# GpSimd adds one more piece of half B's sum of squares at three norm boundaries, and TensorE sums one source one step later

## The chip, the cores and the metric

The kernel runs on one core of a Trainium2 chip. The metric is the device time of one launch in microseconds. Before the change the median of 3 runs is 1094.82 us, and the runs lie between 1094.5 and 1095.06 us.

## The reference, cut to what matters

Two transformer-like layers work on 512 tokens of width 1024. Each layer is a mixer (a recurrent branch with stick-breaking attention in layer 0, windowed attention in layer 1) and a gated conv-FFN. Every one of the four has a norm before it and a norm behind it, so that between two of them stands this pair:

```python
x = x + rms_norm(m, norm_mix_post[layer])
h = rms_norm(x, norm_ffn_pre[layer])
...
def rms_norm(x, g):
    y = xf * lax.rsqrt(jnp.mean(xf * xf, axis=-1, keepdims=True) + RMS_EPS) * g
```

The change touches only the mean of squares of `m`, the output of a mixer or an FFN, for the second half of the tokens.

## The kernel before, in words

Activations lie transposed: 8 tiles (`DT`) of 128 features by 512 tokens (`T`). Every product of activations and weights is done as three matmuls (high by high, low by high, high by low part, lines 1673 to 1675). ScalarE makes the high part of a weight block (`w_hi`, L725), VectorE the low part (`w_lo`, L1122, a subtraction of two SBUF tiles of 128x2048).

There are three boundaries (`bi` = 0, 1, 2): behind mixer 0, behind FFN 0 and behind mixer 1. Boundary 0 lies at about 185 to 237 us of the span, boundary 1 at 540 to 603 us, boundary 2 at 700 to 751 us. At each, the tokens are worked in two halves of 256, A and B, so that half A's norm runs while TensorE still computes half B's last matmuls. Half B's norm then runs while TensorE starts the next projection on half A (`first_units`: two units `j` = 0, 1 of eight steps `k`, six 256-column matmuls a step, first for half A, which I call phase A, then for half B, phase B, which goes through `k` with both units in a step of twelve matmuls).

The chain of half B's norm is this, with the line in brackets:

1. ScalarE squares the last block of half B as two pieces of 256 columns: the lower feature tile into `sq[:, 0:HALF]` (L750, counted by `psq_done`), the upper one into `sq[:, HALF:T]` (L751, counted by `psq_last`). Both hold the same 256 tokens.
2. GpSimd adds the lower piece to the running sum `sumsq` (L692, counted by `psum_done`). In half A it adds the upper piece as well (L696; at boundary 2 VectorE does half A's two adds).
3. TensorE sums over the 128 features with a column of ones (L1750). In half B it takes two sources for each of two token blocks, `sumsq` and the upper piece of `sq`: four matmuls. They stand ahead of step 5 of unit 0 in phase A.
4. ScalarE takes the root (L757), VectorE the reciprocal (L1153), and builds a diagonal matrix (L1156). TensorE spreads it with a matmul of ones (L1760) ahead of step 7 of unit 0.
5. VectorE splits a weight block (L1122; at boundary 1 two half blocks of L1128 around the reciprocal), then for each feature tile normalises (L1443), adds to `x` (L1449) and, with ScalarE's `hx_hi` (L941), makes `hx_lo` (L1453). TensorE's phase B waits for `hx_lo` of each `k`.

Ahead of item 4's reciprocal, VectorE's program has another split of a weight block (L1122 with `splits[0]`) at boundaries 0 and 2. Engines take their instructions in program order; the order here is written out by hand.

Of the kernel before, what the change touches and what calls it, by code (L numbers as in the profile page):

```python
# [17 lines left out]
ALU = mybir.AluOpType  # L18
# [3 lines left out]
P = 128  # L22
T = 512
# [36 lines left out]
HALF = T // 2  # L60
# [9 lines left out]
def group_of(u):  # L70

    shift = 0
    for layer in range(2):
        if u >= U_DOWN[layer] + N_DOWN:
            shift += G_SHIFT
        elif u >= U_DOWN[layer]:
            return U_DOWN[layer] - shift + (u - U_DOWN[layer]) // len(DOWN_K)
    return u - shift
# [18 lines left out]
def post_squares(bi):  # L97

    return 8 * bi


def post_sums(bi):

    return (0, 12, 12 + 8)[bi]


def last_square(bi, h):

    return 6 + h if bi == 1 else 4 + 3 * h


def pre_sums(p):

    return (DT - 1) * p


def a_halves(bi):

    return (0, 3, 4)[bi]
# [7 lines left out]
def evacuated(g):  # L127

    return g + 1 - N_IN if g < G_QKV else g + 1 - N_IN - N_QKV
# [24 lines left out]
def build(nc, io, out):  # L154
    es = ExitStack()

    def sem(name):
        return es.enter_context(nc.semaphore(name))
# [5 lines left out]
    def at(name, shape, dt, offset):  # L164
        return nc.alloc_sbuf_tensor_at(name, shape, dt, offset=offset)
# [11 lines left out]
    def place(name, shape, dt):  # L177
        t = at(name, shape, dt, where[0])
        where[0] += size(shape, dt)
        return t  # L180
# [17 lines left out]
    ident, ones = (const[:, P * i:P * i + P] for i in range(2))  # L198
# [17 lines left out]
    sumsq = place("sumsq", [P, T], F32)  # L216
# [16 lines left out]
    sq = [at(f"sq{b}", [P, T], F32, tmp0 + (0, 2, 3)[b] * T * 4) for b in range(3)]  # L233
# [105 lines left out]
    def bank(b, n=1):  # L339
        return ps[:, T * b:T * (b + n)]  # L340
# [18 lines left out]
    def tokens_of(h):  # L359

        return slice(HALF * h, HALF * h + HALF)
# [37 lines left out]
    def sb_set(h):  # L399
# [21 lines left out]
    psq_done, psum_done, pms_mm, pstd_done, prcol_done, pdiag_done, pbc_mm = (sem(n) for n in (  # L421
        "psq_done", "psum_done", "pms_mm", "pstd_done", "prcol_done", "pdiag_done", "pbc_mm"))
    ahalf_mm, ahalf_evac = sem("ahalf_mm"), sem("ahalf_evac")
    psq_last = sem("psq_last")
# [226 lines left out]
    @block.gpsimd  # L651
    def _(pool):
        def pre_norm(p):

            for i in range(1, DT):
                pool.wait_ge(sq_done, DT * p + i + 1)
                if i == 1:
                    if p:
                        pool.wait_ge(pms_mm, 2 * p)
                    ins = pool.tensor_tensor(sumsq[:], sq[0][:], sq[1][:], ALU.add)  # L660
                else:
                    pool.wait_ge(sum_done, pre_sums(p) + i - 1)
                    ins = pool.tensor_tensor(sumsq[:], sumsq[:], sq[i % 2][:], ALU.add)
                ins.then_inc(sum_done, 1)

        def whole_sums(bi, n):

            for i in range(1, n):
                pool.wait_ge(psq_done, post_squares(bi) + i + 1)
                if i == 1:  # L670
                    pool.wait_ge(ms_mm, bi + 1)
                    ins = pool.tensor_tensor(sumsq[:], sq[0][:], sq[1][:], ALU.add)
                else:
                    pool.wait_ge(psum_done, post_sums(bi) + i - 1)
                    ins = pool.tensor_tensor(sumsq[:], sumsq[:], sq[i % 3][:], ALU.add)
                ins.then_inc(psum_done, 1)

        def half_sums(bi, h):

            for j in range(2):  # L680
                q = 2 + 3 * h + j
                pool.wait_ge(psq_done, post_squares(bi) + q + 1)
                for b in range(2):
                    pool.wait_ge(psum_done, post_sums(bi) + 1 + 6 * h + 2 * j + b)
                    pool.tensor_tensor(sumsq[:, tokens_of(h)], sumsq[:, tokens_of(h)], sq[q % 3][:, tokens_of(b)], ALU.add).then_inc(psum_done, 1)

        def last_sum(bi, h):

            q = last_square(bi, h)
            pool.wait_ge(psq_done, post_squares(bi) + q + 1)  # L690
            pool.wait_ge(psum_done, post_sums(bi) + (5 + 2 * h if bi == 1 else 5 + 6 * h))
            pool.tensor_tensor(sumsq[:, tokens_of(h)], sumsq[:, tokens_of(h)], sq[q % 3][:, 0:HALF], ALU.add).then_inc(psum_done, 1)  # L692
            if h == 0:
                pool.wait_ge(psq_last, 2 * bi + 1)
                pool.wait_ge(psum_done, post_sums(bi) + 6)
                pool.tensor_tensor(sumsq[:, 0:HALF], sumsq[:, 0:HALF], sq[q % 3][:, HALF:T], ALU.add).then_inc(psum_done, 1)  # L696

        pre_norm(0)
        whole_sums(0, 2)
        half_sums(0, 0)  # L700
        last_sum(0, 0)
        half_sums(0, 1)
        last_sum(0, 1)
        pre_norm(1)
        whole_sums(1, 6)
        last_sum(1, 0)
        last_sum(1, 1)
        pre_norm(2)
        whole_sums(2, 2)
        half_sums(2, 0)  # L710
        half_sums(2, 1)
        last_sum(2, 1)
        pre_norm(3)
# [956 lines left out]
    def _(pe):  # L1670
# [6 lines left out]
        def unit_ready(u, i=None):  # L1677

            pe.wait_ge(w_lo_done, u + 1 if i is None else i * RING + (u + 1))
# [56 lines left out]
        def post_mean_square(bi, h):  # L1736

            if h:
                pe.wait_ge(pstd_done, 2 * bi + 1)
            else:  # L1740
                pe.wait_ge(std_done, bi + 1)
            pe.wait_ge(psum_done, post_sums(bi) + (7 + h if bi == 1 else 7 + 5 * h))
            if h:
                pe.wait_ge(psq_last, 2 * bi + 2)
            q = last_square(bi, h)
            for t in (2 * h, 2 * h + 1):
                c = P * (t - 2 * h)
                srcs = (sumsq[:, P * t:P * t + P], sq[q % 3][:, HALF + c:HALF + c + P])[0:h + 1]
                for i, src in enumerate(srcs):
                    last = pe.matmul(bank(7)[:, t:t + 1], src, ones[:, 0:1], start=i == 0 and t == 2 * h, stop=i == h and t == 2 * h + 1)  # L1750
            last.then_inc(pms_mm, 1)

        def post_spread(bi, h):

            pe.wait_ge(pdiag_done, 2 * bi + h + 1)
            if h:
                pe.wait_ge(pstd_done, 2 * bi + 2)
            elif bi == 2:
                pe.wait_ge(ahalf_evac, a_halves(2) + 3)
            pe.matmul(bank(6 + h)[:, 0:HALF], ones, diag[:, 2 * h:2 * h + 2, :].rearrange("p t c -> p (t c)"),  # L1760
                      start=True, stop=True).then_inc(pbc_mm, 1)
# [190 lines left out]
        def first_half(u, h, k):  # L1952

            for b in range(2):
                dst = bank(group_banks(group_of(u)) + h)[:, tokens_of(b)]
                ins = three(dst, *weights(u, k, b), hx_hi[:, k, tokens_of(h)], hx_lo[:, k, tokens_of(h)], k == 0 and b == 0,
                            k == UK - 1 and b == 1)
            return ins
# [82 lines left out]
        def first_units(bi, u):  # L2041

            a_copied, evac = a_halves(bi) + (1 if bi == 1 else 3), evacuated(group_of(u) - 1)
            pe.wait_ge(ahalf_evac, a_copied)
            for j in range(2):
                unit_ready(u + j)
                for k in range(UK):
                    if j == 0 and k == 5:
                        post_mean_square(bi, 1)
                    if j == 0 and k == 7:  # L2050
                        post_spread(bi, 1)
                    pe.wait_ge(hx_ready, DT + 2 * DT * bi + k + 1)
                    first_half(u + j, 0, k)
            pe.wait_ge(group_evac, evac)
            for k in range(UK):
                pe.wait_ge(hx_ready, 2 * DT + 2 * DT * bi + k + 1)
                for j in range(2):
                    last = first_half(u + j, 1, k)
                    if k == UK - 1:
                        last.then_inc(unit_done, 1)  # L2060
            if bi == 1:
                banks_free(group_of(u + 2))
                unit_ready(u + 2)
                tokens(u + 2, group_banks(group_of(u + 2)),
                       {(0, 2): lambda: mean_square(2), (1, 4): lambda: spread(2)}).then_inc(unit_done, 1)
            else:
                unit(u + 2, hx, hooks={(0, 1): lambda: mean_square(bi + 1), (0, 6): lambda: spread(bi + 1)})
# [147 lines left out]
        ffn(0, 0)  # L2215
        down_halves()
        first_units(1, U_QKV)
        unit(U_QKV + 3, hx)
        unit(U_QKV + 4, hx, hooks={
# [119 lines left out]
```

## Time and profile before

| What | Value |
|---|---|
| median of 3 runs | 1094.82 us |
| profiled execution, device time | 1095.11 us |
| its span in the trace | 1093.3 us |
| TensorE matmul busy | 1083.1 us, 99% of the span |
| VectorE busy | 691.2 us, 63% |
| ScalarE busy | 501.8 us, 46% |
| GpSimd busy | 69.9 us, 6%, 62 instructions |
| granted TensorE clock | 1.00 of full speed over the span |

The profiled execution is 1.81 us longer than its span and 0.29 us above the median. A matmul's row begins when it starts and its length includes the pipeline's drain, so the distance from start to start is what a matmul costs the engine. A record on the row of TensorE is one pass: these float32 matmuls of one column show two records each.

### The profile page before, as it was taken

Reading aid. Unit: us, or ns where it says so; the run is one execution under the profiler, and the core shown is the slowest. Engines: PE = TensorE matmul, PEld = TensorE weight load, DVE = VectorE, ACT = ScalarE, POOL = GpSimd, SP = SyncE. Lnnn points to the kernel's source line nnn. Section 1 sums busy time; section 2 is a strip of 40 time slices with the busy share of each in tenths; the row PEclk is TensorE's granted clock in tenths of the full one; section 3 lists DMA queues with packets and bytes.
Section 4 is the critical chain, followed back from the end, with each engine's and each line's share of the span. In section 5 each row is a group of like instructions: output and inputs, shape, how many; then the busy total and the mean of one; then the engine's idle time right before and its main releaser. Section 6 shows DMA issues by size and latency. Waiting matters only on the chain.

```text
span 1093.3 us, 15107 instructions
## 1 busy us (share of the span) xinstructions
PE 1083.1 (99%) x5998; PEld 918.3 (84%) x5998; DVE 691.2 (63%) x920; ACT 501.8 (46%) x714; POOL 69.9 (6%) x62
## 2 busy tenths in 40 slices
PE   9999999999999999999999999999999999999997
PEld 7886889998888888888899877998888888888886
DVE  7675777788776767622257777398876767661313
ACT  6556966555343444322235466454444444441321
POOL 3000001230000000001103000121000000000000
PEclk9999999999999999999999999999999999999999
DMA  6323232213222222223322623212222222221322
GB/s 230 116 78 77 78 116 78 78 43 112 82 111 86 106 89 103 83 91 106 107 81 82 166 94 116 83 73 78 85 108 89 104 92 100 97 96 58 116 97 77
DMA packets 22919, 105.49 MB, mean 96 GB/s; under 512 B 4048, under 2 KB 6480, under 8 KB 12240
## 3 DMA queue, kind: packets, MB, share of 16 engines
q1 hardware_dynamic: 22720, 104.71, 28.1%
q8 instruction: 40, 0.66, 0.2%
q14 instruction: 15, 0.12, 0.0%
q10 hardware_dynamic: 144, 0.01, 0.0%
HBM read 98.02 MB, written 2.10 MB: 92 GB/s over the span
## 4 chain that ended last, share of the span: by engine, by line
PE 92%; DVE 4%; ACT 2%; DMA 1%; issue 1%; SPq 1%; DVEq 0%
PE ps L1673 29%; PE ps L1675 28%; PE ps L1674 28%; PE ps L1856 1%; PE ps L1869 1%; PE ps L1892 1%; DVE ps L1443 1%; PE ps L2162 1%; DVE x L1449 1%; PE ps L2173 1%; DVE hx_lo L1453 1%; DVE w_lo L1169 1%; PE ps L2189 1%; ACT w_hi_s L725 1%; ACT prob L1075 0%
## 5 line engine op out<-in xcount | busy, mean ns | idle before, releaser
L1673 PE MATMUL ps<-hx_hi,w_hi 128*128 128x512 f32 x812 | 320.0, 394 | 1.0 <-DVE w_lo L1169 0.9
L1675 PE MATMUL ps<-hx_hi,w_lo 128*128 128x512 f32 x812 | 316.4, 390 | 0.0
L1674 PE MATMUL ps<-hx_lo,w_hi 128*128 128x512 f32 x812 | 316.3, 390 | 0.0
L1122 DVE TENSOR_TENSOR w_lo<-w_raw,w_hi 128x2048 fp32r<-128x2048 f32 (+1 forms) x74 | 167.7, 2266 | 122.1 <-ACT w_hi L725 121.9
L725 ACT ACTIVATE w_hi<-w_raw 128x2048 fp32r<-128x2048 f32 (+1 forms) x76 | 142.0, 1870 | 109.0 <-DMA w_raw<-in_ffn_w_down 90.7
L1673 PEld LDWEIGHTS ps<-hx_hi,w_hi 128*128 128x128 f32 x812 | 152.4, 188 | 38.0 <-issue 6.5
L1675 PEld LDWEIGHTS ps<-hx_hi,w_lo 128*128 128x128 f32 x812 | 152.4, 188 | 31.9
L1674 PEld LDWEIGHTS ps<-hx_lo,w_hi 128*128 128x128 f32 x812 | 152.5, 188 | 31.0 <-issue 0.5
L984 ACT ACTIVATE cg<-ug,vec 128x512 f32<-128x512 f32 x44 | 35.9, 816 | 140.7 <-DVE ug L1489 140.7
L996 ACT ACTIVATE g_hi<-cv 128x512 f32 (+1 forms) x44 | 27.8, 632 | 111.1 <-DVE cv L1507 111.1
L1498 DVE SCALAR_TENSOR_TENSOR cg<-ug,vec,cg 128x511 f32<-128x511 f32 x88 | 65.8, 748 | 20.4 <-ACT cg L984 20.4
L1489 DVE TENSOR_TENSOR ug<-ps,rbc 128x512 f32<-128x512 f32 x44 | 30.4, 690 | 61.4 <-PE ps L1675 61.3
L1673 PE MATMUL ps<-w_hi,g_hi 128*128 128x512 f32 x176 | 68.9, 391 | 0.0
L1675 PE MATMUL ps<-w_hi,g_lo 128*128 128x512 f32 x176 | 68.5, 389 | 0.0
L1674 PE MATMUL ps<-w_lo,g_hi 128*128 128x512 f32 x176 | 68.5, 389 | 0.0
L1498 DVE SCALAR_TENSOR_TENSOR cv<-uv,vec,cv 128x511 f32<-128x511 f32 x88 | 65.8, 748 | 0.0
L1509 DVE TENSOR_TENSOR g_lo<-cv,g_hi 128x512 f32 (+1 forms) x44 | 30.5, 693 | 37.0 <-ACT g_hi L996 37.0
L1674 PE MATMUL ps<-g_lo,w_hi 128*128 128x512 f32 x132 | 51.4, 389 | 0.0
L1675 PE MATMUL ps<-g_hi,w_lo 128*128 128x512 f32 x132 | 51.4, 389 | 0.0
L1673 PE MATMUL ps<-g_hi,w_hi 128*128 128x512 f32 x132 | 51.4, 389 | 0.0
L941 ACT ACTIVATE hx_hi<-x,vec 128x256 fp32r<-128x256 f32 x48 | 24.0, 506 | 33.9 <-DVE x L1449 33.9
L1675 PEld LDWEIGHTS ps<-w_hi,g_lo 128*128 128x128 f32 x176 | 33.0, 188 | 6.9
(284 smaller groups left out, 1948.9 us busy)
## 6 DMA issues: line engine op xcount, KB each, us to landing
w_raw<-in_ffn_w_up SPq DMA_DIRECT2D x40, 1024.0 KB, 4.8
w_raw<-in_ffn_w_down SPq DMA_DIRECT2D x16, 1024.0 KB, 4.8
w_raw<-in_even_w_in SPq DMA_DIRECT2D x6, 1024.0 KB, 4.9
w_raw<-in_even_w_out SPq DMA_DIRECT2D x3, 1024.0 KB, 4.8
w_raw_s<-in_odd_w_qkv SPq DMA_DIRECT2D x3, 1024.0 KB, 4.8
w_raw<-in_odd_w_qkv SPq DMA_DIRECT2D x3, 1024.0 KB, 5.4
w_raw<-in_odd_w_o SPq DMA_DIRECT2D x3, 1024.0 KB, 5.4
rsw<-rp SPq DMA_DIRECT2D x40, 64.0 KB, 2.0
```

What stands on the lines that cost most here:

```text
L725: act.activation(w_hi[buffer(u)][:, 0:k], w_raw[buffer(u)][:, 0:k], ACT.Copy).then_inc(w_hi_done, 1)
L941: act.activation(hx_hi[:, i, tokens_of(h)], x[:, i, tokens_of(h)], ACT.Identity, scale=gain(which, layer, i)).then_inc(hx_hi_done, 1)
L984: act.activation(cg[:], ug[:], ACT.Identity, scale=col(ffn_vec(layer, 2, j)), bias=col(ffn_vec(layer, 3, j))).then_inc(center, 1)
L996: act.activation(tile_(g_hi, j), cv[:], ACT.Copy).then_inc(g_hi_done, 1)
L1122: dve.tensor_tensor(w_lo[s][:, 0:k], w_raw[s][:, 0:k], w_hi[s][:, 0:k], ALU.subtract).then_inc(w_lo_done, 1)
L1169: dve.tensor_tensor(w_lo[u][:, ks], w_raw[u][:, ks], w_hi[u][:, ks], ALU.subtract).then_inc(piece_signal(n, first_lo, w_lo_done), 1)
L1489: dve.tensor_tensor(halves(ug[:]), out_tile(u, b0, 0), halves(rbc[:]), ALU.mult).then_inc(scaled, 1)
L1498: dve.scalar_tensor_tensor(out=dst[:, s:], in0=src[:, 0:T - s], scalar=col(ffn_vec(layer, 2 - s, j + FT * b)), in1=dst[:, s:], op0=ALU.mul ...
L1509: dve.tensor_tensor(tile_(g_lo, j), cv[:], tile_(g_hi, j), ALU.subtract).then_inc(g_ready, 1)
L1673: pe.matmul(dst, s_hi, r_hi, start=first, stop=False)
L1674: pe.matmul(dst, s_hi, r_lo, start=False, stop=False)
L1675: return pe.matmul(dst, s_lo, r_hi, start=False, stop=last)
```

## The change

In half B, too, GpSimd adds the upper piece of the last square to `sumsq`, at all three boundaries. TensorE then sums only `sumsq`, with two matmuls where there were four, and no longer waits for `psq_last`; it waits for one more GpSimd add. The counts in `post_sums` follow. The sum is moved from ahead of step 5 to ahead of step 6 of unit 0, the spread from ahead of step 7 of unit 0 to ahead of step 0 of unit 1.

```diff
 def post_sums(bi):
-    return (0, 12, 12 + 8)[bi]
+    return (0, 13, 13 + 9)[bi]
...
-            if h == 0:
-                pool.wait_ge(psq_last, 2 * bi + 1)
-                pool.wait_ge(psum_done, post_sums(bi) + 6)
-                pool.tensor_tensor(sumsq[:, 0:HALF], sumsq[:, 0:HALF], sq[q % 3][:, HALF:T], ALU.add).then_inc(psum_done, 1)
+            pool.wait_ge(psq_last, 2 * bi + h + 1)
+            pool.wait_ge(psum_done, post_sums(bi) + (6 + 2 * h if bi == 1 else 6 + 6 * h))
+            pool.tensor_tensor(sumsq[:, tokens_of(h)], sumsq[:, tokens_of(h)], sq[q % 3][:, HALF:T], ALU.add).then_inc(psum_done, 1)
...
-            pe.wait_ge(psum_done, post_sums(bi) + (7 + h if bi == 1 else 7 + 5 * h))
-            if h:
-                pe.wait_ge(psq_last, 2 * bi + 2)
-            q = last_square(bi, h)
+            pe.wait_ge(psum_done, post_sums(bi) + (7 + 2 * h if bi == 1 else 7 + 6 * h))
             for t in (2 * h, 2 * h + 1):
-                c = P * (t - 2 * h)
-                srcs = (sumsq[:, P * t:P * t + P], sq[q % 3][:, HALF + c:HALF + c + P])[0:h + 1]
-                for i, src in enumerate(srcs):
-                    last = pe.matmul(bank(7)[:, t:t + 1], src, ones[:, 0:1], start=i == 0 and t == 2 * h, stop=i == h and t == 2 * h + 1)
+                last = pe.matmul(bank(7)[:, t:t + 1], sumsq[:, P * t:P * t + P], ones[:, 0:1], start=t == 2 * h, stop=t == 2 * h + 1)
...
-                    if j == 0 and k == 5:
+                    if j == 0 and k == 6:
                         post_mean_square(bi, 1)
-                    if j == 0 and k == 7:
+                    if j == 1 and k == 0:
                         post_spread(bi, 1)
```

On TensorE, at boundary 2, phase A, the sum stood after five steps of unit 0. Steps of unit 0 read `w_hi_x_148`; the rows below are the last matmul of step 4, the sum, and the first of step 5:

```order
L1675 MATMUL ps<-hx_hi,w_lo_x_146 128x256
L1750 MATMUL ps<-const,sumsq 128x1
L1750 MATMUL ps<-const,sq_86 128x1
L1750 MATMUL ps<-const,sumsq 128x1
L1750 MATMUL ps<-const,sq_86 128x1
L1673 MATMUL ps<-hx_hi,w_hi_x_148 128x256
```

Now six steps of unit 0 stand ahead of it, and it has two matmuls, which the print joins in one row (lines are seven lower in the changed file from here on, and one lower for the three matmuls of a product):

```order
L1674 MATMUL ps<-hx_hi,w_lo_x_146 128x256
L1743 MATMUL ps<-const,sumsq 128x1 x2
L1672 MATMUL ps<-hx_hi,w_hi_x_148 128x256
```

The six matmuls of step 5 have moved ahead of the sum, and the two with `sq_86` are gone.

The spread, on the same engine and at the same boundary, stood ahead of step 7, the last one of unit 0 (`w_hi_x_148`), with unit 1 (`w_hi_s_154`) behind it:

```order
L1760 MATMUL ps<-diag,const 128x256
L1673 MATMUL ps<-hx_hi,w_hi_x_148 128x256
L1674 MATMUL ps<-hx_lo,w_hi_x_148 128x256
L1675 MATMUL ps<-hx_hi,w_lo_x_146 128x256
L1673 MATMUL ps<-hx_hi,w_hi_x_148 128x256
L1674 MATMUL ps<-hx_lo,w_hi_x_148 128x256
L1675 MATMUL ps<-hx_hi,w_lo_x_146 128x256
L1673 MATMUL ps<-hx_hi,w_hi_s_154 128x256
```

Now unit 1 begins right behind it:

```order
L1672 MATMUL ps<-hx_hi,w_hi_x_148 128x256
L1673 MATMUL ps<-hx_lo,w_hi_x_148 128x256
L1674 MATMUL ps<-hx_hi,w_lo_x_146 128x256
L1753 MATMUL ps<-diag,const 128x256
L1672 MATMUL ps<-hx_hi,w_hi_s_154 128x256
```

Both pieces have two steps, twelve matmuls, between the sum and the spread, as before. On GpSimd, at boundaries 1 and 2 half B's second add follows the first directly (`sumsq` is the running sum, `sq_86` the buffer of the last square; L660 begins the next norm's sum):

```order
 L692 TENSOR_TENSOR sumsq<-sumsq,sq_86 128x256
+L695 TENSOR_TENSOR sumsq<-sumsq,sq_86 128x256
 L660 TENSOR_TENSOR sumsq<-sq_85,sq_86 128x512
```

VectorE's, ScalarE's and the queues' orders are as before.

## Rows read from the trace of the kernel before

**Rows 1.** The page, part 1: busy time, share of the span, instructions.
```profile
PE 1083.1 (99%) x5998; PEld 918.3 (84%) x5998; DVE 691.2 (63%) x920; ACT 501.8 (46%) x714; POOL 69.9 (6%) x62
```
**Rows 2.** Windows, 716 to 724 us: busy us and instructions by engine, clock, DMA.
```profile
716.00:724.00 8.00, 8.00 (x71) 8.00 (x70) 7.37 (x17) 6.27 (x13) 2.28 (x3) 1.00 0.38 131
```
**Rows 3.** Timeline, TensorE, boundary 0: start, length, engine, line, operation, tiles [idle before].
```profile
210.98 0.35 PE L1750 MATMUL ps<-const,sumsq 128*128 128x1 f32 x2
...
211.87 0.36 PE L1673 MATMUL ps<-hx_hi,w_hi_x 128*128 128x256 f32 x1
...
227.18 0.28 PE L1673 MATMUL ps<-hx_hi,w_hi_x 128*128 128x256 f32 x1
```
**Rows 4.** Timeline, GpSimd, boundary 0, both halves' last adds.
```profile
192.47 0.74 POOL L692 TENSOR_TENSOR sumsq<-sumsq,sq 128x256 f32<-128x256 f32 x1 [2.62 <-ACT sq L750]
193.35 0.74 POOL L696 TENSOR_TENSOR sumsq<-sumsq,sq 128x256 f32<-128x256 f32 x1
...
208.08 2.80 POOL L692 TENSOR_TENSOR sumsq<-sumsq,sq 128x256 f32<-128x256 f32 x1 [1.32 <-ACT sq L750]
```
**Rows 5.** Timeline, VectorE, boundary 0, half B.
```profile
208.00 2.28 DVE L1122 TENSOR_TENSOR w_lo_s<-w_raw_s,w_hi_s 128x2048 fp32r<-128x2048 f32 x1
212.34 0.17 DVE L1153 RECIPROCAL rcol<-std 128x2 f32<-128x2 f32 x1 [2.06 <-ACT std L757]
...
226.15 0.77 DVE L1453 SCALAR_TENSOR_TENSOR hx_lo<-x,vec,hx_hi 128x256 fp32r<-128x256 f32 x1
```
**Rows 6.** Timeline, ScalarE, boundary 0, the root of half B.
```profile
212.04 0.26 ACT L757 ACTIVATE std<-ps,narrow 128x2 f32<-128x2 f32 x1 [1.47 <-PE ps L1750]
```
**Rows 7.** Timeline, TensorE, boundary 1: the sum, the spread, phase B's k = 5.
```profile
576.23 0.28 PE L1750 MATMUL ps<-const,sumsq 128*128 128x1 f32 x2
...
578.77 0.70 PE L1760 MATMUL ps<-diag,const 128*128 128x256 f32 x2
...
592.74 0.28 PE L1673 MATMUL ps<-hx_hi,w_hi_s 128*128 128x256 f32 x1
```
**Rows 8.** Timeline, VectorE, boundary 1: reciprocal, diagonal, `hx_lo` of k = 5.
```profile
578.04 0.16 DVE L1153 RECIPROCAL rcol<-std 128x2 f32<-128x2 f32 x1
578.23 0.48 DVE L1156 TENSOR_SCALAR diag<-const,rcol 128x128 f32<-128x128 f32 x2
...
590.00 0.70 DVE L1453 SCALAR_TENSOR_TENSOR hx_lo<-x,vec,hx_hi 128x256 fp32r<-128x256 f32 x1
```
**Rows 9.** Timeline, GpSimd, boundary 1, half B's last add.
```profile
574.38 0.77 POOL L692 TENSOR_TENSOR sumsq<-sumsq,sq 128x256 f32<-128x256 f32 x1 [15.95 <-ACT sq L750]
```
**Rows 10.** Timeline, GpSimd, boundary 2, half B's last add.
```profile
723.26 0.77 POOL L692 TENSOR_TENSOR sumsq<-sumsq,sq 128x256 f32<-128x256 f32 x1 [1.15 <-ACT sq L750]
```
**Rows 11.** Timeline, VectorE, boundary 2: split, reciprocal, `hx_lo` of k = 4 and 5.
```profile
723.35 2.83 DVE L1122 TENSOR_TENSOR w_lo_s<-w_raw_s,w_hi_s 128x2048 fp32r<-128x2048 f32 x1
726.10 0.15 DVE L1153 RECIPROCAL rcol<-std 128x2 f32<-128x2 f32 x1
...
737.86 1.26 DVE L1453 SCALAR_TENSOR_TENSOR hx_lo<-x,vec,hx_hi 128x256 fp32r<-128x256 f32 x1
...
739.89 0.76 DVE L1453 SCALAR_TENSOR_TENSOR hx_lo<-x,vec,hx_hi 128x256 fp32r<-128x256 f32 x1
```
**Rows 12.** Timeline, TensorE, boundary 2: sum, spread, phase B's k = 4 and 5.
```profile
724.12 0.35 PE L1750 MATMUL ps<-const,sumsq 128*128 128x1 f32 x2
...
726.82 0.70 PE L1760 MATMUL ps<-diag,const 128*128 128x256 f32 x2 [0.15 <-DVE diag L1156]
...
739.17 0.39 PE L1673 MATMUL ps<-hx_hi,w_hi_x 128*128 128x256 f32 x1
...
740.71 0.38 PE L1673 MATMUL ps<-hx_hi,w_hi_x 128*128 128x256 f32 x1
```
**Rows 13.** Timeline, GpSimd and VectorE near the span's start, both busy.
```profile
16.01 1.56 POOL L663 TENSOR_TENSOR sumsq<-sumsq,sq 128x512 f32<-128x512 f32 x1
...
16.34 1.78 DVE L1173 SCALAR_TENSOR_TENSOR hx_lo<-x,vec,hx_hi 128x512 fp32r<-128x512 f32 x1
```

## The prediction

> **What bounds the kernel now.** I read four views in this order. First the busy times [rows 1]: TensorE is busy 99% of the span, so an edit pays only if it removes TensorE time or a TensorE stall, and costs whatever it makes TensorE wait. Second a stretch of TensorE alone, for its pace: 71 matmuls of 256 columns in 8.00 us at full granted clock, 0.113 us each, so a step of six is 0.68 us [rows 2]. Third TensorE's timeline at each boundary, for distances from start to start; only one wait is marked in brackets there, 0.15 us ahead of the spread at boundary 2 [rows 12], but the distances show smaller and unmarked gaps. Fourth the timelines of GpSimd, VectorE and ScalarE there, because half B's norm is a chain through all of them that TensorE meets again in phase B, at each k of `hx_lo`. The question at each boundary is which comes last in phase B, TensorE itself or that chain. The chain's clock starts at the end of the sum.
>
> At boundary 2 it is the chain: `hx_lo` of k = 4 ends at 737.86 + 1.26 = 739.12 [rows 11] and TensorE's k = 4 starts at 739.17; `hx_lo` of k = 5 ends at 740.65, TensorE starts it at 740.71 [rows 12]. At boundary 0 it is TensorE by a little: `hx_lo` of k = 5 ends at 226.92 and could be used 0.05 later, 226.97 [rows 5], TensorE starts k = 5 at 227.18 [rows 3], so the chain has 0.21 us of room. At boundary 1 it has 592.74 - (590.70 + 0.05) = 1.99 us [rows 7, 8].
>
> **What goes from TensorE.** Four matmuls take from 210.98 to 211.87, 0.89 us [rows 3], or 0.22 each. Two go at each of three boundaries: 0.45 us less each. Phase A's steps cost 0.68 us each [rows 2], two of them 1.36.
>
> **What the move does.** Standing one step later and being 0.45 shorter, the sum ends 0.68 - 0.45 = 0.23 us later if nothing makes it wait. The spread, two steps behind it, is due 0.23 later too, with one more step done. Nothing on the queues moves, no DMA is issued at another place.
>
> **What GpSimd's add costs.** It is off TensorE, but TensorE now waits for it. The same pair of adds in half A: 192.47, then 193.35, 0.74 us long [rows 4], so the second starts 0.14 after the first ends and adds 0.88. But GpSimd and VectorE stand in each other's way when both read two SBUF tiles. Near the start, GpSimd's add takes 1.56 us and VectorE's `hx_lo` from 16.34 takes 1.78 and ends at 18.12, 0.55 after the add ends at 17.57 [rows 13]: one at a time. At boundary 0 the half-B add starts at 208.08, 0.08 behind a VectorE split of 2.28 us, and takes 2.80 instead of 0.74; it ends at 210.88, 0.60 after the split [rows 4, 5]. At boundary 2 the add wins by 0.09 and takes 0.77; the split behind it takes 2.83 instead of 2.28 [rows 10, 11]: it could begin about 0.55 late, near 723.90, and holds GpSimd off to its end at 726.18.
>
> **Boundary 0.** First add ends 210.88 (as before). Second: 211.02 to 211.76; VectorE is idle for 2.06 us ahead of 212.34 [rows 5], so nothing blocks it. TensorE starts a sum 0.10 us after the add's end (210.88 to 210.98) [rows 3, 4]: 211.86. Without the wait it would start at 210.98 + 0.68 = 211.66. So it waits 0.2, is through at 212.31, where before its next step 6 began at 211.87 + 0.68 = 212.55: TensorE is 0.24 ahead. The root before began at 212.04, 1.06 after the sum's start [rows 6]; with two matmuls fewer it follows 0.61 after the start: 212.47, 0.43 later. Reciprocal, diagonal, split, normalising and `hx_lo` follow 0.43 later; the second add ends before the diagonal is built and meets no two-tile work of VectorE. The chain had 0.21 of room at k = 5, so TensorE leaves phase B 0.43 - 0.21 = 0.22 later. **+0.22 us.**
>
> **Boundary 1.** First add 574.38 to 575.15 [rows 9], second to 576.03; TensorE comes at 576.23 + 0.68 = 576.91 [rows 7], so it does not wait. The root starts at 576.91 + 0.61 (worked out at boundary 0) = 577.52 and is usable 0.30 after (212.04 to 212.34) [rows 5, 6], at 577.82. The reciprocal stands directly behind a half split of VectorE, with no idle time, at 578.04 [rows 8], so it stays. Diagonal ready at 578.71, spread before at 578.77 [rows 7, 8]. Before, TensorE came there after two steps (576.23 + 0.89 + 1.36 = 578.48) and stood 0.29. Now it comes at 576.91 + 0.45 + 1.36 = 578.72 and spreads at the same 578.8 with a whole step more done. So it gains 0.68, with 1.99 of room for the chain in phase B, and keeps it. **-0.68 us.**
>
> **Boundary 2.** First add ends 724.03, the second is issued about 724.17, while the split has held since 723.90. By the row of boundary 0 it ends 0.60 after the split: 726.78; TensorE starts the sum at 726.88, where before it started at 724.12 [rows 12] and now was due at 724.80. Behind it on TensorE waits all of phase A's rest: it stands 2.1 us. Root at 726.88 + 0.61 = 727.49, reciprocal 0.30 later, 727.79, against 726.10 [rows 11]: +1.69. VectorE, ready at 726.18, stands still until then with the whole chain behind. The spread is due at 726.88 + 0.45 + 1.36 = 728.69, behind the diagonal (0.18 + 0.48 after the reciprocal, as in [rows 8]: 728.45), so the 0.15 us wait there goes; it pays nothing, since phase B's k = 4 and k = 5 hang on the chain. Its `hx_lo` move by 1.69, TensorE's k = 5 from 740.71 to 742.40. **+1.69 us.**
>
> What TensorE gains in phase A (0.45 and the spread's wait) is used up there.
>
> **The sum.** 0.22 - 0.68 + 1.69 = +1.23 us. On the profiled execution 1095.11 + 1.23 = 1096.34; that execution is 0.29 above the median, so on the median 1094.82 + 1.23 = 1096.05, say 1096.0 us. I take 0.2% as what a measurement can tell from no change, here 2.2 us; the forecast is a small loss inside it.
>
> The unknown is the grant: no row shows two adds of GpSimd with a 2.28 us split issued between them. Lower bound for boundary 2: the second add is not held up at all (0.88 as in half A); upper: held up for the whole of the split. Rows 13, where the two engines alternate although GpSimd's next add is ready, are the nearest, and they say held up. I take the upper one.
>
> Two pages bear on this. The Trainium skill (SBUF — State Buffer, Who interferes with whom) says that whichever of the two engines issues first holds their common port pair for the whole instruction. By that, as by the rows, the split issued at 723.35 goes ahead of an add issued at 724.17. The Trainium skill (Perfetto Trace Analysis, GPSIMD Engine Instruction) warns that a GpSimd row's length is unreliable and to go by spacing. By spacing an add costs 0.88 where the row says 0.74; TensorE's start 0.10 behind the drawn end shows that the ends can be used here.
>
> **Rivals.**
> - *No port trouble at boundary 2.* GpSimd's second add slips in or beside: ends 724.91, TensorE sums at 725.01, 0.2 late; the root follows at 725.62 as before, the chain does not move, boundary 2 gives 0. If in addition the add at boundary 0 is only 0.2 late as worked out, the sum is 0.22 - 0.68 + 0 = -0.46: 1094.4 us, on the faster side though within 0.2%. For it: the two adds are only 0.14 apart. Against: rows 13 and the split's 0.55 us stretch.
> - *The add goes first, the split pays.* Same 725.01 for the sum, but the split is held until about 724.8 and ends at 727.0 instead of 726.18: chain +0.85 at boundary 2. Sum +0.4: 1095.2 us. It needs GpSimd to take the port twice running over a waiting VectorE, which rows 13 speak against.
> - *Boundary 1's gain is lost.* Between boundaries 1 and 2 other engines end the attention steps; if one of them does not move along with TensorE, the 0.68 goes and the sum is +1.9: 1096.7. Against: everything there starts from TensorE's results behind the boundary.
> - *The stall costs clock.* The granted clock is 1.00, 2.4 GHz, ahead of boundary 2 [rows 2]. If 2.1 us of standing made it fall to 1.2 GHz, each 0.113 us matmul would cost 0.113 more: 20 of them add 2.3 us and bring 1098.3. No row shows a stall of that length, for or against.
>
> **How the numbers follow.** Forecast 0.68; no port trouble 0.11; split pays 0.07; gain of boundary 1 lost 0.09; clock 0.05. The forecast's own range is 1095.6 to 1096.5. Adding the first two on one side and the third on the other, and 0.3 us for the spread of the runs, the range is 1094.7 to 1097.1. Faster by over 0.2% would need -2.2 us, more than the three boundaries can give (3 x 0.68): 0.02. Slower by over 0.2% (above 1097.0) takes the clock case and the upper tail of the others: 0.12. The rest, 0.86, is within 0.2%.
>
> **What would show each step.** At boundary 2 GpSimd's second add of half B some 2.5 us long, ending 0.6 behind the split; a TensorE wait of some 2 us on it ahead of the sum; VectorE idle about 1.6 us ahead of its reciprocal. At boundary 0 the root about 0.43 later counted from its half-B first square. At boundary 1 no gap ahead of the spread. Counted from boundary to boundary, TensorE's distance should be +0.2, -0.7, +1.7. If the second add at boundary 2 is 0.74 us long, the forecast is wrong and the first two rivals decide.

## The result, and the profile after

The changed kernel takes 1098.34 us in the median of 8 runs (1097.84 to 1100.28), the kernel before 1095.0 us (1094.5 to 1095.58, 8 runs): ratio 1.0032, interval [1.0022, 1.0043], 3.3 us slower. Measured once more beside the kernel before, it is 1098.89 against 1095.27 us (1.0035, [1.0021, 1.0048]). The forecast was 1096.0 us and the range ended at 1097.1, so the time lies outside it.

The page after; it answers to [rows 1]. The span is 3.1 us longer, TensorE is busy 0.2 us less, GpSimd 4.1 us more:

```profile
span 1096.4 us, 15086 instructions
PE 1082.9 (99%) x5986; PEld 918.0 (84%) x5986; DVE 691.3 (63%) x920; ACT 502.2 (46%) x714; POOL 74.0 (7%) x65
```

So much of the loss is waiting. Some of it must be slower matmuls, though: six one-column matmuls are gone, by the forecast 3 x 0.45 us, and the busy time fell by 0.2. TensorE's waits after, whole span (in total, times, longest, us):

```profile
PE ps L1743 <- POOL sumsq L695: 2.2, 2, 2.0
...
PE ps L1672 <- DVE w_lo_s L1121: 1.0, 1, 1.0
PE ps L1753 <- DVE w_lo_s L1127: 0.9, 1, 0.9
...
PE ps L1672 <- DVE hx_lo L1452: 0.4, 1, 0.4
```

Four new ones. The first two numbers of the first line are one wait of 2.0 at boundary 2 and one of 0.2 at boundary 0, on the added add. The second and third lines are both at boundary 1, which the prediction had as a gain. The fourth, 0.37 us, is at boundary 0, in phase B at k = 4 (225.93).

**Boundary 2.** GpSimd, VectorE and TensorE after, three timelines (start, length, instruction, idle before). They answer to [rows 10 to 12]; the whole place has come 0.76 us later:

```profile
724.02 0.76 POOL L692 TENSOR_TENSOR sumsq<-sumsq,sq 128x256 f32<-128x256 f32 x1 [1.16 <-ACT sq L749]
724.93 2.59 POOL L695 TENSOR_TENSOR sumsq<-sumsq,sq 128x256 f32<-128x256 f32 x1
```

```profile
724.11 2.83 DVE L1121 TENSOR_TENSOR w_lo_s<-w_raw_s,w_hi_s 128x2048 fp32r<-128x2048 f32 x1
728.57 0.17 DVE L1152 RECIPROCAL rcol<-std 128x2 f32<-128x2 f32 x1 [1.64 <-ACT std L756]
```

```profile
727.66 0.58 PE L1743 MATMUL ps<-const,sumsq 128*128 128x1 f32 x4 [2.00 <-POOL sumsq L695]
...
731.19 0.41 PE L1672 MATMUL ps<-hx_hi,w_hi_s 128*128 128x256 f32 x1
```

The added add is 2.59 us long and ends at 727.52, 0.58 behind the split's end at 726.94. The reciprocal moves from 726.10 to 728.57, which is 1.71 later counted from the first add. The last row shows what I had given a chance of 0.05: some 2 us behind the stall a 256-column matmul takes 0.41 us in its row, and they start 0.21 apart, not 0.113. The windows after show the clock (stretch, its length, busy of TensorE, weight loads, VectorE, ScalarE, GpSimd, then granted clock, DMA):

```profile
728.00:730.00 2.00, 2.00 (x16) 2.00 (x16) 1.39 (x4) 0.26 (x1) 0.00 (x0) 0.86 0.00 0
730.00:732.00 2.00, 2.00 (x9) 1.81 (x9) 1.97 (x3) 0.00 (x0) 0.00 (x0) 0.50 0.03 8
732.00:734.00 2.00, 2.00 (x16) 2.00 (x15) 1.93 (x5) 1.66 (x4) 0.00 (x0) 0.78 0.00 0
```

0.50 is 1.2 GHz: 9 matmuls in 2 us, where [rows 2] has 71 in 8.

**Boundary 1.** VectorE and TensorE after; they answer to [rows 7, 8]:

```profile
579.07 1.22 DVE L1127 TENSOR_TENSOR w_lo_s<-w_raw_s,w_hi_s 128x1024 fp32r<-128x1024 f32 x1
581.08 0.49 DVE L1442 SCALAR_TENSOR_TENSOR ps<-m,vec,ps 128x256 f32<-128x256 f32 x1 [0.79 <-PE ps L1753]
...
594.81 3.38 DVE L1121 TENSOR_TENSOR w_lo_s<-w_raw_s,w_hi_s 128x2048 fp32r<-128x2048 f32 x1
```

```profile
580.34 0.70 PE L1753 MATMUL ps<-diag,const 128*128 128x256 f32 x2 [0.87 <-DVE w_lo_s L1127]
...
598.34 0.35 PE L1672 MATMUL ps<-w_hi_s,hx_hi 128*128 128x256 f32 x1 [0.96 <-DVE w_lo_s L1121]
```

The spread is not waiting for the diagonal. It waits for a weight block, because "ahead of step 0 of unit 1" is written behind `unit_ready(u + j)` of unit 1, and the last half of those weights' low part is made by the half split at 579.07, which comes after the diagonal. VectorE in turn waits 0.79 us for the spread.

**Boundary 0.** The added add takes 0.73 us, and the reciprocal, at 212.34 in [rows 5], is 0.50 later:

```profile
211.05 0.73 POOL L695 TENSOR_TENSOR sumsq<-sumsq,sq 128x256 f32<-128x256 f32 x1
```

```profile
212.84 0.17 DVE L1152 RECIPROCAL rcol<-std 128x2 f32<-128x2 f32 x1 [2.53 <-ACT std L756]
```

### The profile page after: what moved, and what is told of

It reads as the page before. It is cut to its first block, busy times and chain, and to the rows that moved or that the text cites. A ratio compares the mean times of both kernels' runs of the same rounds, so it can differ in the third digit from the quotient of the medians.

```text
span 1096.4 us, 15086 instructions
## 1 busy us (share of the span) xinstructions
PE 1082.9 (99%) x5986; PEld 918.0 (84%) x5986; DVE 691.3 (63%) x920; ACT 502.2 (46%) x714; POOL 74.0 (7%) x65
## 4 chain that ended last, share of the span: by engine, by line
PE 90%; DVE 5%; ACT 2%; issue 1%; DMA 1%; POOL 1%; SPq 1%; DVEq 0%; POOLq 0%
PE ps L1672 28%; PE ps L1674 27%; PE ps L1673 27%; DVE ps L1442 1%; DVE hx_lo L1452 1%; DVE x L1448 1%; PE ps L1849 1%; PE ps L1862 1%; PE ps L1885 1%; PE ps L2155 1%; PE ps L2166 1%; DVE w_lo L1168 1%; DVE w_lo_s L1121 1%; PE ps L2182 1%; ACT w_hi_s L724 1%
## 5 line engine op out<-in xcount | busy, mean ns | idle before, releaser
L672 POOL TENSOR_TENSOR sumsq<-sq,sq 128x512 f32<-128x512 f32 x3 | 4.2, 1398 | 518.5 <-ACT sq L752 518.5
```

## Where the time is lost, by stretch

For every traced kernel I took two starts at each boundary, half B's first add on GpSimd (L692) and the next norm's sum on TensorE (first matmul of L1733 in the kernel before), and compared their distance with that in the kernel before (24.04, 23.40 and 22.35 us). The attention column runs from boundary 1's second start to the first square of boundary 2 (103.13 us before); no kernel here changes an instruction in it. Each value is from one profiled execution, in us against before; the last column is the difference of the medians, from 11 runs unless said.

| kernel | boundary 0 | boundary 1 | attention | boundary 2 | medians |
|---|---|---|---|---|---|
| the change | +0.40 | +0.91 | -0.59 | +2.31 | +3.34 (8 runs) |
| the change again | +0.40 | +0.93 | +0.04 | +1.76 | +3.62 (5 runs) |
| e1, boundary 0 only | +0.24 | | -0.49 | | +0.11 |
| e2, boundary 1 only | | +0.93 | -0.45 | | +0.64 |
| e3, boundary 2 only | | | +0.16 | +1.75 | +2.02 |
| e4, boundary 2, late sum | | | -0.66 | +1.78 | +1.53 |
| e5, boundary 1, spread first | | +0.01 | -0.19 | | -0.07 |
| e6, boundary 2, split halved | | | -0.56 | +0.67 | +0.92 |
| e7, move without add | +0.23 | +1.21 | -0.55 | +0.01 | +1.34 |
| e8, add without move | +0.25 | +0.04 | -0.22 | +3.58 | +3.81 (5 runs) |
| e9, repaired | +0.24 | +0.03 | +0.96 | +0.02 | +0.32 |
| e10, add goes first | | | -0.15 | +1.07 | +1.52 |
| e11, half split later | | | +0.43 | -0.16 | +0.52 |

The empty cells are stretches whose program is that of before; they read between -0.01 and +0.04, but for boundary 0 in e5 (-0.24) and e6 (-0.18), so a single value of 0.2 at boundary 0 proves little by itself; there the five kernels that have the change or a part of it all read +0.23 to +0.40.

These differences go with something that no edit here makes: at a granted clock of 1.00, TensorE runs its 256-column matmuls at one of two paces. The same stretch of boundary 0 in the kernel before and in e5, which has the same program there:

```profile
216.00:224.00 8.00, 8.00 (x71) 8.00 (x69) 7.79 (x15) 5.21 (x10) 4.08 (x4) 1.00 0.00 0
```

```profile
216.00:224.00 8.00, 8.00 (x73) 8.00 (x72) 7.79 (x15) 5.22 (x10) 3.94 (x4) 1.00 0.00 0
```

From start to start a matmul takes 0.118 us in the first and 0.113 us in the second and in e6. Over this half the quick pace brings TensorE up to the chain of the norm and gains it about the chain's 0.21 us of room. It also parts +0.40 from +0.24 where the program is the same: from the wait at k = 4 to the next norm's sum the change takes 6.60 us at the slow pace, e1 6.44 us at the quick one. What sets the pace stays open.

The attention stretch moves by -0.66 to +0.96 between executions of the same instructions. There TensorE waits for a chain of small DMAs. The chain that ended last has this last landing in the kernel before and after (start, us, what):

```profile
666.35 3.16 DMA rsw<-rp
```

```profile
667.72 2.54 DMA rsw<-rp
```

Up to the start of that landing the two traces take the same time from boundary 1's second start (68.57 and 68.60 us), so the 0.62 us between the landings is the 0.59 that the profile after seems to give back. In the change again the stretch reads +0.04, so it is luck of one execution, not an effect of the change, and the boundaries have to be read apart.

## The experiments

**e1, e2, e3: one boundary each.** The count of `post_sums`, the add, the one-source sum and the places are those of the change for one value of `bi` and those of before for the others:

```diff
-            if h == 0:
+            if h == 0 or bi in (2,):
...
-                    if j == 0 and k == 5:
+                    if (j, k) == {0: (0, 5), 1: (0, 5), 2: (0, 6)}[bi]:
```

> The change made at boundary 0 alone. Theory: the second add lies behind a first add that a VectorE split holds up, so half B's sum ends about 0.5 us later, the chain of the norm follows 0.5 us later, and 0.1 to 0.2 us of that is room: +0.3 to +0.4 us against before, no lower granted clock. Rival (each boundary costs a third of the measured 3.3 us, as a price of the change itself): +1.1 us.

> The change made at boundary 1 alone. Theory: the spread now stands behind TensorE's wait for unit 1's weights, whose low part VectorE finishes only after the diagonal; chain +0.9 us and the first matmul of the third unit, which waits for the last split of the chain, +0.9; the attention stage behind it may give back up to 0.6 where a DMA of the rotary swap lands earlier: +0.3 to +1.0 us. What the prediction said of this boundary: -0.7 us. Rival (a third each): +1.1 us.

> The change made at boundary 2 alone. Theory: the second add is held up by the split (2.6 us long instead of 0.74), TensorE stands 2 us, the chain is 1.7 us later, and the clock that drops behind the stall costs another 0.6 us: +2.1 to +2.6 us, with a stretch of a few us at half the granted clock near 727 to 731 us. Without the clock's share it would be +1.7. Rival (a third each): +1.1 us.

Measured: 1095.24, 1095.77 and 1097.15 us against 1095.13, so +0.1, +0.6 and +2.0; ratios 1.0002 [0.9993, 1.0011], 1.0005 [0.9996, 1.0014] and 1.0019 [1.0010, 1.0028]. Only the third is clear by its interval; for the first two the trace has to speak, and it shows +0.24 and +0.93 at the boundaries named and nothing at the others. By the traces thirds of 1.1 us are out; the medians' intervals alone would allow them. The medians add to 2.8 us against the 3.3 and 3.6 of the whole, within what the intervals allow; the stretches without any loss of clock add to 0.40 + 0.92 + 1.76 = 3.1.

In e3 TensorE stood 2.0 us on the add as in the change, but the clock stayed up in this execution:

```profile
728.00:730.00 2.00, 2.00 (x17) 1.94 (x16) 1.89 (x4) 0.04 (x1) 0.00 (x0) 1.00 0.03 8
730.00:732.00 2.00, 2.00 (x20) 2.00 (x19) 1.93 (x4) 0.15 (x1) 0.00 (x0) 1.00 0.00 0
```

So the expectation of a stretch at half clock was wrong for this execution, and boundary 2 costs 1.75 without it, against 2.31 with it. TensorE itself lost more than that 0.56 in the trace of the change: its first matmul of phase B starts 13.08 us behind half B's first add, in e3 11.48, so the slow stretch cost it 1.6 us. But in e3 it then stands about 1.0 us in waits for the norm's chain, which is equally late in both traces. That much of the loss is hidden.

**e4: the same add, the sum where TensorE has work.** Boundary 2 alone; sum ahead of step 1 of unit 1, spread ahead of step 3:

```diff
+                    if (j, k) == {0: (0, 5), 1: (0, 5), 2: (1, 1)}[bi]:
...
+                    if (j, k) == {0: (0, 7), 1: (0, 7), 2: (1, 3)}[bi]:
```

> At boundary 2 alone, GpSimd's second add as in the change, but the sum stands ahead of step 1 of unit 1 and the spread ahead of step 3, so that TensorE has work while the add is held up. Theory: no stall over 0.3 us, granted clock 1.00 throughout, the sum starts at the same 726.9 us and the chain is 1.7 us late as before: +1.5 to +1.8 us, so 0.6 less than the change at boundary 2 alone; that difference is the clock's share. Rival (the clock costs nothing that the chain does not cost anyway): the same as the change at boundary 2 alone, within 0.2 us. Rival (the stall itself, not the chain, is the cost): near 0.

Measured 1096.66 us, +1.5 (1.0015 [1.0006, 1.0024]). The add on GpSimd is as long as ever:

```profile
723.56 2.60 POOL L696 TENSOR_TENSOR sumsq<-sumsq,sq 128x256 f32<-128x256 f32 x1
```

TensorE now has no wait on it, but the missing time turns up in phase B, as three waits for `hx_lo`, 1.3 us in all, and the boundary costs +1.78, what it cost in e3. The stall itself is not the price: a stall that is filled is paid again where the chain is met. The medians of the two differ by 0.5 us, which is the size expected for the clock's share, but with these intervals the medians do not show it.

The mean clock of a run says little here. It is 1.000 or 0.999 in e4's 11 runs and 0.997 or 0.998 in nine of e3's 11, but the profiled execution of e3 has 0.998 with no fall at boundary 2: its clock falls at 1091.8 us, behind the last matmul, where it costs nothing:

```profile
1092.00:1094.00 2.00, 0.00 (x0) 0.00 (x0) 0.85 (x2) 0.00 (x0) 0.00 (x0) 0.50 0.48 180
```

That end stretch takes 0.00 to 0.16% off the mean in the 14 traces. Means of 0.997 and less stand only in kernels whose TensorE stalls for 2 us or more, four times in e3's 11 runs. That speaks for falls at boundary 2 in those executions, but no trace of them shows it.

**e5: the spread ahead of the weights at boundary 1.**

```diff
             for j in range(2):
+                if j == 1 and bi == 1:
+                    post_spread(bi, 1)
                 unit_ready(u + j)
```

> Boundary 1 alone, with the spread put ahead of TensorE's wait for unit 1's weights, everything else as in the change. Theory: the spread starts at 578.8 us as before the change, the chain does not move, and TensorE's gain of 0.7 us in phase A ends in a longer wait at the third unit, whose weights VectorE splits at the end of the chain with 0.1 us of room: 0 us against before, within 0.2. Rival (the prediction's own view, room of 2 us, gain kept): -0.7 us.

Measured 1095.21 against 1095.28 us (1.0000 [0.9991, 1.0009]); boundary 1 +0.01. TensorE's timeline there:

```profile
579.75 0.39 PE L1673 MATMUL ps<-hx_hi,w_hi_s 128*128 128x256 f32 x1 [0.43 <-DVE w_lo_s L1128]
...
596.87 0.35 PE L1673 MATMUL ps<-w_hi_s,hx_hi 128*128 128x256 f32 x1 [0.51 <-DVE w_lo_s L1122]
```

Two things are shown. The +0.93 of the change at boundary 1 is the place of the spread behind the wait for weights, since moving that one call takes it away. And my gain of 0.68 does not exist: what TensorE saves comes back as two waits for split weights. In the kernel before, the third unit began at 597.01, and the split that feeds it ended at 596.87, so there was 0.1 us of room, not 1.99:

```profile
593.50 3.37 DVE L1122 TENSOR_TENSOR w_lo_s<-w_raw_s,w_hi_s 128x2048 fp32r<-128x2048 f32 x1
```

**e6: VectorE's split at boundary 2 in two halves.**

```diff
+                    if bi == 2:
+                        split_lo_part(splits[0], 0, UK // 2)
+                        split_lo_part(splits[0], UK // 2, UK)
```

> The change at boundary 2 alone, and VectorE's 2.28 us split ahead of the reciprocal cut in two of half the size. Theory (one engine at a time on two SBUF inputs, the waiting one goes next): the second add gets in after the first half, about 1.7 us long instead of 2.6, TensorE stands 0.9 us instead of 2.0, no fall of the clock, chain 0.7 us late: +0.5 to +0.9 us against before. Rival (GpSimd waits for VectorE to run out of two-input work): as the change at boundary 2 alone, +2.3 us.

Measured 1096.2 against 1095.28 us, +0.9 (1.0012 [1.0003, 1.0021]); boundary 2 +0.67. GpSimd gets in between the halves:

```profile
723.61 1.52 POOL L696 TENSOR_TENSOR sumsq<-sumsq,sq 128x256 f32<-128x256 f32 x1
```

1.52 us instead of 2.60, and VectorE's two halves take 3.43 us together, where the whole split took 2.83 [rows 11]: VectorE pays 0.6 us for the add that got in between, and its reciprocal comes 0.64 late. TensorE's wait is 0.9 us. The two engines take turns at the grain of an instruction.

**e7 and e8: the two parts of the change, all boundaries.** e7 keeps two sources and has only the places moved; e8 has the add and one source at the old places.

> All three boundaries: the sum and the spread one step later, but still two sources on TensorE and no new add of GpSimd. Theory: chain 0.68 us late at boundary 0 less 0.2 of room (+0.5); boundary 1 as in the change, since the spread stands behind the weights (+0.3 to +1.0); boundary 2, where VectorE's split hides about 0.2 of it: +0.4 to +0.5. In all +1.3 to +2.0 us, no lower clock. Rival (the add is what costs, the move nothing): within 0.3 us of before.

> All three boundaries: GpSimd's add and the one-source sum, at the old places. Theory: boundary 0 the sum waits 0.9 us for the add, chain +0.43 to 0.5, +0.3; boundary 1 the add ends at 576.0 ahead of the sum at 576.23, chain hidden, spread not behind the weights: 0; boundary 2 the sum waits 2.7 us for the add that the split holds up, chain +1.7, clock falls, +2.3 or a little more. In all +2.5 to +3.0 us, so boundary 1's share is what is missing against the change. Rival (the move is what costs): within 0.5 us of before.

e7: 1096.62 us, +1.3 (1.0016 [1.0007, 1.0025]). e8: 1099.09 us, +3.8 (1.0036 [1.0023, 1.0050]). Both rivals fall: each part costs, at its own boundary. The move costs +1.21 at boundary 1 and nothing at boundary 2, where I had expected 0.4 to 0.5: the sum starts 0.6 us later there, and that is hidden behind VectorE's split. The add costs +3.58 at boundary 2 and 0.04 at boundary 1. e8 costs more than I expected: without the move TensorE stands 2.7 us, and its clock falls sooner and in a stretch full of steps:

```profile
728.00:730.00 2.00, 2.00 (x10) 2.00 (x11) 1.50 (x4) 0.26 (x1) 0.00 (x0) 0.50 0.00 0
730.00:732.00 2.00, 2.00 (x14) 1.95 (x13) 1.85 (x3) 0.00 (x0) 0.00 (x0) 0.76 0.03 8
```

That is 3.58 - 1.76 = 1.8 us more than boundary 2 costs without a fall, and not all of it is clock. From 732 us to the end of the boundary TensorE runs at 0.118 us from start to start, in e3 at 0.113; over some 140 matmuls this makes about 0.6 us, an estimate, and leaves about 1.2 for the clock. Over e8's five runs the mean clock and the time go together: 1097.53 us at 1.000, 1098.37 and 1099.09 at 0.998, 1099.61 at 0.997, 1100.36 at 0.996.

**e9: the change repaired.** No added add at boundary 2, the spread of boundary 1 ahead of the weights; the moved places and boundary 0 and 1's adds stay.

> The change with its two costly pieces taken out: no added GpSimd add at boundary 2 (TensorE sums two sources there, one step later), and at boundary 1 the spread ahead of the wait for unit 1's weights. Theory: boundary 0 +0.3, boundary 1 0, boundary 2 0 (the split hides the move): +0.3 us against before, within 0.3. Rival (something else in the change costs, in TensorE's order or the counts): over +1 us.

Measured 1095.57 against 1095.25 us, +0.3 (1.0000 [0.9990, 1.0009]). The stretches read +0.24, +0.03, +0.02. Beyond boundary 0's 0.24 nothing else in the change costs.

**e10: VectorE lets both adds go first at boundary 2.**

```diff
+                    if bi == 2:
+                        dve.wait_ge(psum_done, post_sums(2) + 13)
                     split_lo(splits[0])
```

> The change at boundary 2 alone, and VectorE's split there waits until GpSimd's second add is done. Theory (the add is long only because the split holds it up): the second add takes 0.74 us, TensorE's sum starts at 725.0 with hardly a wait, the split runs from 725.0 to 727.2 and the reciprocal is about 1.0 us late: +0.8 to +1.1 us, clock 1.00. Rival (the add is slow for a reason of its own): the add still takes over 1.5 us.

```profile
723.87 0.74 POOL L696 TENSOR_TENSOR sumsq<-sumsq,sq 128x256 f32<-128x256 f32 x1
```

```profile
724.64 2.29 DVE L1122 TENSOR_TENSOR w_lo_s<-w_raw_s,w_hi_s 128x2048 fp32r<-128x2048 f32 x1 [1.52 <-POOL sumsq L696]
726.85 0.16 DVE L1153 RECIPROCAL rcol<-std 128x2 f32<-128x2 f32 x1
```

The add takes 0.74 us, and TensorE waits 0.16 us for it: it was long for nothing but the split. The boundary still costs +1.07, because now the split and the reciprocal behind it are 1.05 late. The median is +1.5 (1.0013 [1.0004, 1.0022]), 0.4 above what I expected; the trace does not show where.

**e11: a try at a faster kernel.** Before's adds and sum; at boundary 2 the spread ahead of unit 1, and the second half of the third unit's split behind the chain:

```diff
+                    if bi == 2:
+                        split_lo_part(splits[1], 0, UK // 2)
...
+            if bi == 2:
+                split_lo_part(splits[1], UK // 2, UK)
             split_lo(splits[2])
```

> No added add; at boundary 2 the split of the third unit's weights is cut in two and its second half is put behind the chain of the norm, and the spread stands ahead of unit 1. Theory: the chain is 1.1 us shorter up to its last step, TensorE no longer waits for it in phase B and loses its wait at the spread, 0.4 to 0.6 us in all, if the last splits are still in time: -0.3 to -0.6 us against before, at the edge of what can be told. Rival (the last splits become the bound): 0 to +0.5 us.

Measured 1095.77 against 1095.25 us (1.0001 [0.9992, 1.0010]); boundary 2 -0.16 in its trace. The chain came 1.1 us earlier and phase B ran without a wait, but the half split put last shared its time with GpSimd, 2.31 us instead of 1.22, and ended 0.14 us ahead of the third unit's first matmul. TensorE came there at the same time, since it ran phase B at the slow pace of 0.118; at the quick one it would have had to wait for the split. The rival held, and no version here beats the kernel before.

**The change again.**

> The change itself once more, beside the kernel before on the same chip. Theory: +2.8 to +3.4 us, the sum of its three boundaries measured apart (0.1 + 0.6 + 2.0 = 2.8) plus what a longer fall of the clock adds in some executions; the slower executions are those with the lower mean granted clock. Rival (the parts do not add up, the three together cost clearly more): over +3.6 us in the median.

Measured 1098.89 against 1095.27 us, +3.6 in five runs, at the edge that I had given the rival; the interval, 2.3 to 5.3 us, tells nothing apart. In its trace the clock stayed up (1.00 in each 4 us stretch behind the stall) and the boundaries read +0.40, +0.93, +1.76, the same sum of 3.1. Its slowest run, 1100.49 us, has the lowest mean clock, 0.996, as the slowest of the first eight has, 1100.28 us; its fastest, 1097.94, has 1.000. But runs in between break the order (1098.3 us at 1.000 against 1097.84 at 0.999), as they would with an attention stretch that moves by itself and a mean that includes the end stretch.

## Why the prediction was wrong, step by step

- *Boundary 2's chain: right.* The two-engine rule gave an add that ends 0.60 behind the split and a chain 1.69 late. Measured 0.58, the reciprocal 1.71 to 1.72 late in three traces (the change, its repeat, e3), and 1.75 and 1.76 for the boundary in the two of them without a fall of the clock. e6 and e10 show the cause, from both sides. The rivals "no port trouble" and "the split pays" are out, though e10 shows the second's price, about 1.0, when it is forced.
- *Boundary 1: the step that failed most.* I wrote "it comes at 576.91 + 0.45 + 1.36 = 578.72 and spreads at the same 578.8 with a whole step more done". I counted matmuls from the order and not the waits between them: the call had moved behind `unit_ready` of unit 1, which the listing of instructions doesn't print and the quoted code does. The sign that I had named, no gap ahead of the spread, failed with a wait of 0.87 us. Result +0.91 to +0.93 for -0.68, an error of 1.6 us out of the 2.1 between forecast and result. At boundaries 0 and 2 the same wait is harmless, since unit 1's split is the one ahead of the reciprocal.
- *Boundary 1's room: also wrong.* "With 1.99 of room for the chain in phase B, and keeps it" looked at `hx_lo` alone. The chain's last link is the split for the third unit, with 0.1 us of room. e5 shows that even with the first error taken out the gain is 0.
- *The clock: a rival that I under-rated in its chance and over-rated in its price.* I gave it 0.05 and 2.3 us, and it came in one of three traces with the 2.0 us stall. TensorE lost 1.6 us of matmul time, and since it had about 1.0 us of room before the chain, 0.6 reached the end (2.31 - 1.75). My 2.3 let every slow matmul reach the end. In e3 and in the repeat it cost nothing, in e8 about 1.2.
- *Boundary 0: small error of size.* +0.24 to +0.40 for +0.22; the reciprocal was 0.50 late for 0.43. The rest is the pace: "71 matmuls of 256 columns in 8.00 us" counts the rows that only reach into the window. In that window the starts are 0.118 apart up to about 721 us and 0.113 behind it, and the room of 0.21 at boundary 0 holds for the slow pace alone.
- *The attention rival*, a lost gain in that stretch, had no gain to lose. That stretch varies by more than any of my terms for boundaries 0 and 1, which my range took in only as 0.3 us of spread.

Put right, the sum without the clock is 0.4 + 0.9 + 1.75 = 3.05 us, and the clock added 0.6 in one trace of the change and nothing in the other. The medians, 3.3 and 3.6 us, lie between.

## What to carry to other kernels

When an instruction is moved, write down every semaphore wait that it now stands behind, not only the instructions; "the same two steps apart" says nothing if a wait lies between. Follow a chain to the last thing that TensorE takes from it, weight splits included, before calling a gain kept. And before giving the idle GpSimd an add, look at what VectorE runs in those microseconds: if it reads two SBUF tiles, one of the two stands for the whole of the other's instruction, and TensorE stands with it.

## What the runs showed of the hardware

- GpSimd's add and VectorE's two-input split exclude each other for whole instructions and take turns: one 256-column add took 0.74 us with VectorE kept out, 1.52 behind a half split and 2.59 behind a whole one. The Trainium skill (SBUF — State Buffer, Who interferes with whom) says that the one that issues first holds the shared pair for the whole instruction and the other fully blocks; these three rows agree.
- After a 2.0 us stall of TensorE the granted clock fell to 0.50 (1.2 GHz) in the trace of the change, 1.8 us after TensorE had gone on, and stayed at 1.00 in e3 and in the repeat. After 2.7 us in e8 it fell 0.2 us after TensorE had gone on. So the same stall has a price that differs from one execution to the next, here 0 and 0.6 us.
- At a granted clock of 1.00 the start-to-start distance of 256-column matmuls is 0.118 us in some stretches and 0.113 in others, and the same program had either from one execution to the next (boundary 0 in the kernel before and in e5). Over a stretch of 140 matmuls that is 0.6 us.
- The last landing of a run of small SBUF-to-SBUF copies took 3.16 us in one execution and 2.54 in another, which is enough to hide or to feign an effect of half a microsecond.
